# A two-layer encoder trunk: the count loaded a quad sooner, the key job moved directly ahead of the branch, and the later rounds as a loop over single quads

## What is computed

```python
h = h + mixed @ w_out[l]
h = h + cross_attention(rms_norm(h, norm_cross[l]), rms_norm(mem, norm_mem[l]), ...)
h = h + hier_moe(rms_norm(h, norm_ffn[l]), ...)

def hier_moe(h, ...):      # top-1 of 4 groups, then top-2 of its 8 experts
    y = 0
    for e in range(32):
        hid = jax.nn.silu(t @ w_gate[e]) * (t @ w_up[e])
        y = y + combine[:, e:e + 1] * (hid @ w_down[e])
```

## Time and profile before

| | us |
|---|---|
| runs | 928.28 to 929.55, median 929.06 |
| the profiled execution, its own time | 926.52 |
| its span | 924.40 |
| TensorE busy | 845.6 (91% of the span) |
| VectorE busy | 286.4 (31%) |
| ScalarE busy | 166.8 (18%) |
| mean granted TensorE clock | 0.972 of full |
| HBM | 270.81 MB read, 294 GB/s over the span |

### The profile page before, as it was taken

The page is one execution under the profiler, slowest core; times in us unless marked ns, Lnnn a source line. Parts: engine busy times, 40 slices in busy tenths (PEclk is TensorE's granted clock), DMA queues, the critical chain, the costliest instruction groups (busy, mean ns, idle before and its releaser), DMA issues.

```text
span 924.4 us, 11875 instructions
## 1 busy us (share of the span) xinstructions
PE 845.6 (91%) x5080; PEld 559.0 (60%) x5080; DVE 286.4 (31%) x587; ACT 166.8 (18%) x387; POOL 15.1 (2%) x21
## 2 busy tenths in 40 slices
PE   7999999999999999875999999999999899877666
PEld 6888875689555455533646887766975544332321
DVE  2427576133253111000103666723123421110011
ACT  2101135412111000000003112451121100000003
POOL 0500000000000000000000000000000000000000
PEclk9999999999999999898999999999999999998798
DMA  9953354284558999999996444408665899999994
GB/s 354 378 182 103 137 183 183 91 311 177 241 215 348 429 425 425 429 427 423 427 426 276 158 163 181 184 1 315 262 274 181 333 430 425 428 426 429 423 428 172
DMA packets 23930, 272.71 MB, mean 295 GB/s; under 512 B 3008, under 2 KB 3392, under 8 KB 5952
## 3 DMA queue, kind: packets, MB, share of 16 engines
q1 hardware_dynamic: 22576, 270.50, 72.0%
q10 hardware_dynamic: 1296, 1.37, 0.5%
HBM read 270.81 MB, written 1.05 MB: 294 GB/s over the span
## 4 chain that ended last, share of the span: by engine, by line
PE 73%; DMA 18%; DVE 3%; issue 2%; ACT 2%; another core or an unknown queue 1%; PEld 0%; DVEq 0%; PEldq 0%; ACTq 0%
PE bank L614 17%; PE bank L690 11%; DMA early<-in_expert_units 11%; DMA ring<-in_expert_units 7%; PE bank L729 7%; PE bank L1040 6%; PE bank L773 4%; PE bank L761 4%; PE bank L716 3%; PE bank L668 3%; PE bank L676 2%; PE bank L1070 2%; PE bank L1051 1%; PE bank L858 1%
## 5 line engine op out<-in xcount | busy, mean ns | idle before, releaser
L614 PE MATMUL bank<-uT,ring 128*128 128x256 f32 x480 | 107.0, 381 | 0.8 <-DVE uT L1551 0.8
L614 PEld LDWEIGHTS bank<-uT,ring 128*128 128x128 f32 x480 | 90.3, 190 | 14.1 <-DVE uT L1551 1.0
L716 PE MATMUL bank<-sel,hn 128*128 128x128 f32 x512 | 65.3, 289 | 19.0 <-issue 18.1
L729 PE MATMUL bank<-ring,xT 128*32 128x512 f32 x576 | 68.7, 618 | 13.9 <-DMA ring<-in_expert_units 13.8
L716 PEld LDWEIGHTS bank<-sel,hn 128*128 128x128 f32 x512 | 63.3, 205 | 21.1 <-issue 21.1
L729 PE MATMUL bank<-early,xT 128*32 128x512 f32 x448 | 57.9, 658 | 18.7 <-DMA early<-in_expert_units 18.7
L773 PE MATMUL bank<-yy,states 128*128 128x512 f32 x128 | 61.8, 608 | 1.5 <-ACT yy L1456 1.5
L1040 PEld LDWEIGHTS bank<-uT,ring 128*128 128x128 f32 x512 | 57.8, 192 | 1.1 <-issue 0.5
L1040 PE MATMUL bank<-uT,ring 128*128 128x128 f32 x512 | 57.8, 275 | 0.0
L690 PE MATMUL bank<-ring,early 128*128 128x512 f32 x128 | 56.6, 592 | 0.0
L690 PE MATMUL bank<-ring,uT 128*128 128x512 f32 x128 | 55.9, 592 | 0.0
(11 more groups left out here) (303 smaller groups left out, 987.2 us busy)
## 6 DMA issues: line engine op xcount, KB each, us to landing
ring<-in_expert_units SPq DMA_DIRECT2D x51, 2048.0 KB, 27.2
early<-in_expert_units SPq DMA_DIRECT2D x43, 2048.0 KB, 32.5
ring<-in_fixed_units SPq DMA_DIRECT2D x16, 2048.0 KB, 8.1
ring<-in_fixed_units SPq DMA_DIRECT2D x25, 1024.0 KB, 17.7
early<-in_expert_units SPq DMA_DIRECT2D x4, 1024.0 KB, 7.9
ring<-in_fixed_units SPq DMA_DIRECT2D x4, 512.0 KB, 4.3
ring<-in_fixed_units SPq DMA_DIRECT2D x2, 768.0 KB, 4.2
early<-in_mem_turned SPq DMA_DIRECT2D x2, 512.0 KB, 5.4
```

Source lines behind the costliest of these rows:

```text
L614: mm = pe.matmul(o[row0:row0 + m], w[:, c, c0:c0 + m], rhs[:, c], start=(c == 0), stop=(c == chunks - 1))
L716: mm = pe.matmul(bank[half][:, c * P:c * P + P], hn[:, t, half * 4 + c], sel[:, t].rearrange("p e s -> p (e s)"), start=(t == 0), stop=(t ...
L729: mm = pe.matmul(bank[2][32 * e:32 * e + 32, :], xT[:, 2 * n + c, 32 * e:32 * e + 32], w[:, e, :, c], start=(n == 0 and c == 0), stop=(n = ...
```

## The change

The diff in full:

```diff
@@ -79,7 +79,7 @@
-QUADS_PER_STEP = 4
+QUADS_PER_STEP = 1
@@ -99,10 +99,11 @@
     out = []
     for q in range(QUADS):
-        out += [(lay, q * UNITS_PER_QUAD + n) for n in range(4)]
+        ups = 6 if q == DRAIN - 1 else 4
+        out += [(lay, q * UNITS_PER_QUAD + n) for n in range(ups)]
         if lay == 0 and q in NEXT_IN_QUAD:
             out.append((1, NEXT_IN_QUAD[q]))
-        out += [(lay, q * UNITS_PER_QUAD + n) for n in range(4, 6)]
+        out += [(lay, q * UNITS_PER_QUAD + n) for n in range(ups, 6)]
     return out
@@ -1145,10 +1146,8 @@
-                def later_rounds(S):
-
-                    pe.wait_ge(E["rounds"], 1)
-                    r = pe.value_load(rounds_i[0:1, 0:1], min_val=1, max_val=8)
+                def later_rounds(S, r):
+
                     with pe.If(r > 1):
@@ -1176,13 +1175,16 @@
                     name = NEXT_IN_QUAD.get(q) if lay == 0 else None
-                    if name is not None:
+                    if name is not None and q + 1 != DRAIN:
                         pe.wait_ge(next_gained, 1)
                         fill_next(name, base)
+                    if q + 2 == DRAIN:
+                        pe.wait_ge(E["rounds"], 1)
+                        r = pe.value_load(rounds_i[0:1, 0:1], min_val=1, max_val=8)
                     if q + 1 == QUADS:
                         last_down_and_scatter(E, base, units_of(q, 4, 6), name)
                     else:
-                        down(E, q, base, units_of(q, 4, 6), name, q + 1 != DRAIN)
+                        down(E, q, base, units_of(q, 4, 6), name if q + 1 != DRAIN else None, q + 1 != DRAIN)
@@ -1190,9 +1192,13 @@
                     if q + 1 == DRAIN:
-                        later_rounds(LATER_ROUNDS[lay])
+                        if name is not None:
+                            fill_next(name, base)
+                        later_rounds(LATER_ROUNDS[lay], r)
                         base = pe.snap(ring_base)
                         gather(E, DRAIN)
+                        if name is not None:
+                            free_unit(name, 1)
@@ -1475,7 +1481,7 @@
-                    if lay == 0 and q in NEXT_IN_QUAD:
+                    if lay == 0 and q in NEXT_IN_QUAD and q + 1 != DRAIN:
                         keep_memory(1, NEXT_IN_QUAD[q])
@@ -1483,6 +1489,8 @@
                     if q + 1 == DRAIN:
+                        if lay == 0:
+                            keep_memory(1, NEXT_IN_QUAD[q])
                         later_rounds(LATER_ROUNDS[lay])
```

## The result

The changed kernel's median over 11 runs is 930.62 us (927.42 to 932.73), against 928.73 for the kernel before (925.87 to 929.56): a ratio of 1.0024, 95% interval 1.0014 to 1.0033. Measured again twice with other runs of before beside it, the ratio was 1.0006 (0.9989 to 1.0024) and 1.0004 (0.9993 to 1.0015). Over all runs of this study the 35 of the changed kernel average 929.1 us and the 122 of before 928.1. The difference is 1.0 us with a standard error of 0.4, or 0.1%, and the first ratio overstates it. The profiled execution of the changed kernel took 927.42 us, the fastest of its eleven, so its trace doesn't show what made the others slower. What is clear is the spread: 11 of the 35 lie above 930.2 us, 3 of the 122 of before.

What follows compares the result with a forecast made beforehand. Both layers' experts were taken to end on the DMA stream: 0 for load, key job and 18.1 us of covered pauses, +1.53 for the clock; 926.52 became 928.05, and the median 929.06 became 930.6 us; range 926.4 to 932.6.

Steps and rivals of the forecast that it cites:

- Rate between 424 and 430: Sign: the queues' load rate stays at 424 to 430 GB/s from 340 to 480 us.
- quad 7's last unit at 473.0 give or take 1.2: Sign: layer 0's last up unit of quad 7 starts at 473.0 us, give or take 1.2.
- a new wait of 2 us: Sign: in layer 0 TensorE newly waits about 2 us before the second half of quad 5's down products.
- key job ending near 430: Sign: layer 0's key job, moved behind the scatter and directly ahead of the branch, ends near 430 us.
- Waits ahead of quad 7's last unit growing to 8.8 us, the 16 matmuls at 473 taking 3.4: Signs, layer 0: data waits grow from 1.3 to about 8.8 us; the last unit's matmuls take 3.4 rather than 1.9.
- Layer 1's last up unit 428 us after layer 0's: Sign: the distance between the two layers' last up units stays at 428 us, as before.
- The branch: Shorter body and key job shrink pauses, freeing TensorE 4 to 9.5 us (layer 0), 0.7 to 8.6 (layer 1); worth 0.
- The clock, +1.53 us: Waits in layer 0's quad 7 drop TensorE's clock; its last 16 matmuls take 3.45, not 1.92 us; bounds 0 and 2.3.
- Layer 1's last unit pays already, 0: Layer 1's last up unit already runs at the lower clock; waits only spread over quad 6; 0, bounds -1.53 and +1.53.
- Fetches, 0 within 1.1: One instruction fetch more or fewer on the slowest DMA engine shifts a layer's end by 0 to 1.1 us; taken 0.
- The key job and the moved load of xk3, 0: Layer 0: key job behind the scatter, xk3's load behind quad 5's two down units; costs 0.
- the release behind the gather, 0: xk3's buffer is released behind quad 6's gather; quad 7's third unit is issued later but lands at 468.05; costs 0.

Runs made afterwards that it cites:

- no_branch: Kernel before, with TensorE's count load, branch and jumped-over loop of later rounds left out in both layers; 926.91 us, ratio 0.9985.
- after_work: Changed kernel with some 7 us of idle matmuls ahead of quad 6's gather in layer 0; 928.65 us, ratio 1.0012.
- after_third: The changed kernel, word for word, run a third time; 929.00 us (925.65 to 930.15).
- after_again: The changed kernel, word for word, run a second time; 927.15 us (925.95 to 934.41).
- before_again: The kernel before, word for word, run again for a second trace; 928.04 us, ratio 1.0004.
- only_body: Kernel before with QUADS_PER_STEP = 1 (loop body of one quad) and nothing else; 930.17 us, ratio 1.0015.
- old_body: Changed kernel with QUADS_PER_STEP put back to 4 (loop body of four quads); 928.24 us, ratio 1.0001.
- the moved sum: First sum-starting matmul moved into TensorE's 0.99 us wait, plus idle matmuls: changed kernel 927.61 us; kernel before, idle matmuls in layer 1 only, 928.42 us.
- before_work: Kernel before with some 7 us of idle matmuls ahead of quad 6's gather in layer 0; 927.93 us, ratio 1.0004.

## Why the prediction came out as it did

The range held, and so did the reading of what ends the experts: the experts end on the data, the chain's issue steps and its 27 us load don't price the branch, and 18 us of pauses are worth nothing that a median shows, at most 0.3%. The unchanged rate and landing times, no_branch and the idle matmuls of after_work show this independently. That the median of the first runs equals the forecast, 930.6, is partly luck: the base of the sum, 929.06, was the median of three runs, 1.0 us above the mean of all 122, and with all runs the change costs 1.0 us, not 1.5 to 1.9.

Point by point:

- *Rate between 424 and 430*, *quad 7's last unit at 473.0 give or take 1.2*, *a new wait of 2 us*, *key job ending near 430*: 424 to 431 GB/s, 473.33, 1.95 us, 431.1 (430.0 without the later start of that trace). Right, but for 1 GB/s in one window.
- *Waits ahead of quad 7's last unit growing to 8.8 us, the 16 matmuls at 473 taking 3.4.* The waits came to 7.15 us, since the slow block was the unit before the last and took its time out of the last wait; the last block took 1.92 us. This sign failed in the first trace and in after_third, and came in part (2.90) in after_again.
- *Layer 1's last up unit 428 us after layer 0's.* It came 429.0 us after, against 428.1 in before. The 0.9 us are those of layer 1's routers (20.91 and 20.00), and before_again has them as well (428.9).
- *The branch.* Right that the pauses shrink, wrong in how. I had the target still fetched and the key job hiding it. In layer 0 the branch takes 0.47 us in the trace after, and only_body shows that this needs the short body alone; that the target was there already fits this, but the traces don't show it. The key job's own share is 2.5 of 4.73 us (old_body). In layer 1 the first pause stays, as bounded (0.7 to 8.6 us freed; 5.0 measured).
- *The clock, +1.53 us.* The mechanism was seen and its weight was too high. Tail 0 is 1.3 to 1.7 us longer in three of five traces in which TensorE waits for quad 7's last units with nothing in between (after_again, no_branch, only_body; not after and after_third), and in none of the nine others. But of the three traces of the changed kernel only one pays. In the other two the clock fell one unit early, under the unit before the last (3.60 and 3.59 us, granted 0.55 and 0.54), where the next wait swallows it. The sum put the full 1.53 in where its own rows paid three times in five.
- *Layer 1's last unit pays already, 0.* Right, tail 1 is 15.7 to 16.0 in both kernels; the waits spread over quad 6 and all of quad 7.
- *Fetches, 0 within 1.1.* Stream 0 is 191.01, 191.03 and 191.48 in the changed kernel, 191.94 and 191.49 in before. A gain of about 0.5 us that I had only as a bound, and whose cause stays open. The terms don't add up to the 1.0 us of all runs: tail 0's 1.65 us in one execution of three or of two, less this gain, gives 0.05 to 0.3. Where the rest comes from isn't shown; the traces are too few to say how often an execution pays.
- *The key job and the moved load of xk3, 0*, *the release behind the gather, 0*: right; nothing landed late. The sooner load of the count was not tried alone.
- *Not foreseen*: the routers' stage, 20.0 to 22.6 us without the moved sum. Between traces of one kernel it varies by up to 2.6 us, more than any stage that the change touches.

## What to carry to other kernels

If a chain of waits holds a load that was issued long before it landed, suspect a queue: subtract what such a load takes with nothing ahead of it before pricing anything that delayed its issue, and look whether the rate ever dips. Time freed on an engine that waits for data turned into waits at once here, and in some executions the clock fell under them, which cost 1.3 to 1.7 us at the end of a stage. Matmuls of no use in front of the last blocks kept the last block at 1.92 us in all four kernels that had them in layer 1. They have to fit into the wait: in layer 0 of the kernel before they didn't, and cost 2.7 us for the 1.3 that they saved.

## What was not expected of the hardware

- A branch over one quad's instructions took 0.36 to 0.87 us in layer 0. In layer 1 it took 3.5 to 6.1 us in most of the same kernels, but 0.42 in after_work, and 6.14, 3.68 and 6.02 in three traces of the one changed kernel. Over four quads' instructions it took 6.1 to 6.5 us in both layers of all six traces that have them. So the length of the body matters; why layer 1 differs from layer 0, and one execution from another, isn't shown.
- Behind the same router matmuls and the same waits the clock was low in some executions and not in others of one kernel: 3.68 or 6.32 us for the same eight matmuls.
- Two medians of the same kernel, over 11 and 12 runs, stood 3.5 us apart; beside their own runs of before they gave 1.0024 and 1.0006, whose intervals overlap. At 0.1 to 0.2% of this kernel a comparison of stages in traces says more than the medians, if a stage is followed back to where it first differs: before_work's was late before the edit began.
